# Interleaving the two halves of a split-precision weight block on the matrix engine

## The reference

```
for i in range(DEPTH):                      # 2 layers
    h = h + 0.5 * swiglu(rms_norm(h, norm_ff1[i]), gate, up, down)   # 1024 -> 2816 -> 1024
    hn = rms_norm(h, norm_mix[i])
    if i % 2 == 0:  # z, xbc, dt, gate, xb = split(hn @ hyb_w_in); SSD and RG-LRU; concat @ hyb_w_out
    ...
    else:           # q, k, v = split(hn @ dif_w_qkv); differential attention; @ dif_w_o
    ...
    h = h + 0.5 * swiglu(rms_norm(h, norm_ff2[i]), gate, up, down)
return rms_norm(h, final_norm)
```

## Time and profile before

| | |
|---|---|
| median of 3 runs | 1106.83 us (1105.61 to 1107.73) |
| the profiled execution: its time | 1106.83 us |
| the profiled execution: its span | 1105.0 us |
| granted clock of TensorE, mean | 0.988 |
| PE busy | 1067.4 us, 97% |
| PEld busy | 950.1 us, 86% |
| DVE busy | 824.6 us, 75% |
| ACT busy | 600.0 us, 54% |
| matmuls | 6671, each with a weight load |

### The profile page before, as it was taken

One profiled execution on the slowest core, in us unless ns is written; L12 is line 12 of the kernel. 1 busy time (PEld: TensorE's weight loads), 2 busy tenths in 40 slices (PEclk: granted clock), 3 DMA queues, 4 the chain that ended last, 5 costly groups with the idle time before them and its releaser, 6 DMA issues.

```text
span 1105.0 us, 18467 instructions
## 1 busy us (share of the span) xinstructions
PE 1067.4 (97%) x6671; PEld 950.1 (86%) x6671; DVE 824.6 (75%) x1157; ACT 600.0 (54%) x915; POOL 152.1 (14%) x149
## 2 busy tenths in 40 slices
PE   6999999998998999999999999999999889999996
PEld 4888888897887998888888888888988788888885
DVE  6888765699898768887666887766589677888753
ACT  5555553574877446555445555543536655555442
POOL 7000011102343330000021000012111050000011
PEclk9999999998999999999999999999999999999998
DMA  8666775454443656667655666675644336667661
GB/s 237 198 194 195 201 207 165 136 150 122 123 119 97 177 167 189 191 190 219 189 165 159 194 194 192 189 220 157 175 132 125 91 104 183 191 192 199 191 196 38
DMA packets 364308, 186.51 MB, mean 169 GB/s; under 512 B 5457, under 2 KB 363985, under 8 KB 364257
## 3 DMA queue, kind: packets, MB, share of 16 engines
q1 hardware_dynamic: 364000, 185.26, 59.0%
q0 software_dynamic: 256, 0.59, 0.2%
HBM read 184.78 MB, written 1.05 MB: 168 GB/s over the span
## 4 chain that ended last, share of the span: by engine, by line
PE 83%; DVE 11%; ACT 3%; issue 2%; DMA 0%; DVEq 0%; ACTq 0%; SPq 0%
PE psum L205 44%; PE psum L208 23%; PE psum L189 4%; PE psum L193 4%; PE psum L190 4%; DVE wlo L178 4%; DVE xn L278 1%; ACT arena L1378 1%; DVE arena L912 1%; PE psum L683 1%; DVE small L1483 1%; DVE arena L1462 0%; ACT xn L269 0%; DVE arena L1505 0%; DVE small L1500 0%
## 5 line engine op out<-in xcount | busy, mean ns | idle before, releaser
L178 DVE TENSOR_TENSOR wlo<-raw,whi 128x1024 fp32r<-128x1024 f32 (+1 forms) x324 | 427.5, 1339 | 62.6 <-ACT whi L173 61.7
L173 ACT ACTIVATE whi<-raw 128x1024 fp32r<-128x1024 f32 (+1 forms) x322 | 352.6, 1112 | 43.7 <-PE psum L193 41.9
L205 PE MATMUL psum<-xn,whi 128*128 128x512 f32 x1408 | 360.0, 396 | 11.5 <-ACT whi L173 7.9
L205 PEld LDWEIGHTS psum<-xn,whi 128*128 128x128 f32 x1408 | 255.4, 190 | 61.9 <-DVE xn L278 8.6
L208 PEld LDWEIGHTS psum<-xn,wlo 128*128 128x128 f32 x1408 | 192.9, 191 | 13.7
L208 PE MATMUL psum<-xn,wlo 128*128 128x256 f32 x1408 | 197.1, 283 | 0.0
L205 PE MATMUL psum<-hid,whi 128*128 128x512 f32 x704 | 172.1, 392 | 0.0
L205 PEld LDWEIGHTS psum<-hid,whi 128*128 128x128 f32 x704 | 128.1, 189 | 24.4 <-DVE hid L462 0.4
L189 PE MATMUL psum<-xn,whi 128*128 128x256 f32 x480 | 125.0, 297 | 0.9 <-DVE xn L278 0.9
L190 PE MATMUL psum<-xn,whi 128*128 128x256 f32 x480 | 120.3, 287 | 0.0
L189 PEld LDWEIGHTS psum<-xn,whi 128*128 128x128 f32 x480 | 93.9, 196 | 5.4 <-issue 3.4
(11 more groups left out here) (195 smaller groups left out, 1048.8 us busy)
## 6 DMA issues: line engine op xcount, KB each, us to landing
raw<-in_ffn_gate SPq DMA_DIRECT2D x88, 512.0 KB, 3.8
raw<-in_ffn_up SPq DMA_DIRECT2D x88, 512.0 KB, 4.0
raw<-in_ffn_down SPq DMA_DIRECT2D x64, 704.0 KB, 4.7
raw<-in_hyb_w_in SPq DMA_DIRECT2D x36, 512.0 KB, 4.2
raw<-in_dif_w_qkv SPq DMA_DIRECT2D x24, 512.0 KB, 4.5
raw<-in_hyb_w_out SPq DMA_DIRECT2D x16, 512.0 KB, 4.8
raw<-in_dif_w_o SPq DMA_DIRECT2D x8, 512.0 KB, 4.3
h<-in_xT SPq DMA_DIRECT2D x2, 512.0 KB, 5.2
```

The costliest lines, as they stand in the source:

```text
L173: act.activation(whi[:, s, 0:k * P], raw[:, s, 0:k * P], ACT.Copy).then_inc(s_whi, 1)
L178: dve.tensor_tensor(wlo[:, s, 0:k * P], raw[:, s, 0:k * P], whi[:, s, 0:k * P].bitcast(F32), ALU.subtract).then_inc(s_wlo, 1)
L205: pe.matmul(acc, hi[:, j, :], x[:, t, :, :], start=start and j == 0, stop=False)
```

## The change

In both functions the two loops over the k tiles become one. Tile by tile, the lo matmul now follows the hi matmul (in `multiply`, the two hi matmuls) of the same tile. One wait stands at the start of the block, for `s_wlo`; the wait for `s_whi` is gone, since the lo half of a block is made from its hi half. The number of matmuls, of weight loads and of their columns is unchanged, and nothing changes on the other engines. The order in which the products are added changes.

```diff
         def multiply(pe, b, s, k, x, k0, acc, start=True, stop=True, need=None, part=None):
-            hi, lo = tile_of(whi, s, k), tile_of(wlo, s, k)
-            pe.wait_ge(s_whi, b + 1)
+            pe.wait_ge(s_wlo, b + 1)
             for j in part or range(k):
                 t = k0 + j
                 if need:
                     need(t)
-                pe.matmul(acc, hi[:, j, :], x[:, t, 0, :], start=start and j == 0, stop=False)
-                pe.matmul(acc, hi[:, j, :], x[:, t, 1, :], start=False, stop=False)
-            pe.wait_ge(s_wlo, b + 1)
-            for j in part or range(k):
-                mm = pe.matmul(acc, lo[:, j, :], x[:, k0 + j, 0, :], start=False, stop=stop and j == k - 1)
+                w_hi, w_lo = tile_of(whi, s, k)[:, j, :], tile_of(wlo, s, k)[:, j, :]
+                pe.matmul(acc, w_hi, x[:, t, 0, :], start=start and j == 0, stop=False)
+                pe.matmul(acc, w_hi, x[:, t, 1, :], start=False, stop=False)
+                mm = pe.matmul(acc, w_lo, x[:, t, 0, :], start=False, stop=stop and j == k - 1)
             if j == k - 1:
                 mm.then_inc(s_blk, 1)

         def multiply_wide(pe, b, s, k, x, k0, acc, start=True, stop=True, need=None):
-            hi, lo = tile_of(whi, s, k), tile_of(wlo, s, k)
-            pe.wait_ge(s_whi, b + 1)
+            pe.wait_ge(s_wlo, b + 1)
             for j in range(k):
                 t = k0 + j
                 if need:
                     need(t)
-                pe.matmul(acc, hi[:, j, :], x[:, t, :, :], start=start and j == 0, stop=False)
-            pe.wait_ge(s_wlo, b + 1)
-            for j in range(k):
-                mm = pe.matmul(acc[:, T:2 * T], lo[:, j, :], x[:, k0 + j, 0, :], start=False,
-                               stop=stop and j == k - 1)
+                w_hi, w_lo = tile_of(whi, s, k)[:, j, :], tile_of(wlo, s, k)[:, j, :]
+                pe.matmul(acc, w_hi, x[:, t, :, :], start=start and j == 0, stop=False)
+                mm = pe.matmul(acc[:, T:2 * T], w_lo, x[:, t, 0, :], start=False, stop=stop and j == k - 1)
             mm.then_inc(s_blk, 1)
```

## The result

The changed kernel takes 1112.95 us (median of 8 executions, 1108.48 to 1117.98) against 1106.76 us before (1105.46 to 1107.75): a ratio of 1.0055 with a 95% interval of 1.0032 to 1.0079. It is slower by half a percent, where 1102.2 us and 0.4% faster was forecast, and 1112.95 lies above the range that was given. Its executions also differ much more among themselves: all 25 that were taken of it ran from 1107.1 to 1118.0. In the changed file, L206 and L207 are the wide hi and lo matmuls, L190 to L192 the narrow ones.

The account below looks back on a forecast made before the run. The prediction took PE's matmul stream, plus a few stalls at stage borders, to bound the kernel. Its terms, -4.9 + 5.1 - 3.3 - 1.0 - 0.5 = -4.6 us, gave 1102.2 us, 0.4% faster, with a range of 1088 to 1110.

Parts of the forecast that it names:

- The stream, wide blocks: Gate, up and down blocks of the ffn phases: a pair costs 0.3466 us when interleaved, 4.9 us less in all.
- settled and settled: Wide pair priced from the hi and lo steps of settled runs: 0.227 + 0.120 = 0.347 us.
- first and first: Wide pair priced from the first step of a hi run and of a lo run: 0.233 + 0.113 = 0.346 us.
- the prediction's own bounds: Wide pair between 0.340 us (14 us less than forecast) and 0.353 us (13.5 us more).
- the rival of the long steps: Every pair of the ffn phases pays hi 0.233 and lo 0.120: 13.5 us more, 1115.7 us; chance 0.20.
- The other two rivals: Wide stream: no change-over cost won back, pair 0.349, 1107.1 us, chance 0.13; short steps, pair 0.340, 1088 us, chance 0.17.
- The stream, narrow blocks: In hyb and att all three matmuls of a tile step by 0.120 in either order: costed at nothing.
- The wait at the start of a block: PE waits for the lo half at the first down blocks of each ffn phase: 5.1 us more, nothing elsewhere.
- Tile waits filled by lo matmuls: Lo matmuls fill activation waits: 3.3 us less at starts of phases, 1.0 us less at the mixers' output blocks.
- The start: First block's lo matmuls go into its activation waits and the second block starts earlier: 0.5 us less.
- The sum: Whole kernel: -4.9 + 5.1 - 3.3 - 1.0 - 0.5 = -4.6 us, 1102.2 us, 0.4% faster.

Follow-up runs that it names:

- profile after: Profiled execution of the changed kernel, to hold against the kernel before: 1112.92 us with a span of 1111.1, 6.1 more than before.
- serp: Against the kernel before, every second block in the loops of the down stages takes all lo, then all hi matmuls: 1105.94 us.
- narrow_only: Against the kernel before, only the narrow function (hyb and att) interleaved, with its wait for the lo half ahead: 1105.12 us, ratio 0.9972.
- wait_only: Matmul order of the kernel before, but each block in both functions waits for its lo half at its start: 1113.99 us, ratio 1.0064.
- borders: Against the kernel before, interleaved only in blocks that wait tile by tile for their activation, first down blocks excepted: 1102.1 us, ratio 0.995.

## Why the prediction was wrong

**The stream, wide blocks: the step that failed.** "Two combinations lie between and agree: settled and settled, 0.227 + 0.120 = 0.347, and first and first, 0.233 + 0.113 = 0.346. I take 0.3466." The step that failed is the choice of one price inside the bounds. The number is exact for one of two paces: 0.3466, gate blocks 2.773, down blocks 3.813, all as forecast. That is in part luck, since the steps of that pattern (233, 117, 231, 112 ns) are those of neither combination; only their sum is. The other pace, 0.3533, is the upper end of the prediction's own bounds, and two stages in three ran at it (22 of the 32 interleaved from their first block on). It holds a step that the settled stream of before doesn't have, a hi step of 241 ns. The reading of that stream was too simple as well: its hi steps are 233, 236, 228, 233 and 231 ns before they settle at 227, so 0.233 was neither the only long step nor the longest. For the profile after, the term is 2 x 44 x (-0.020) + 2 x 44 x 0.033 + 4 x 16 x 0.054 = +4.6 us, where -4.9 stood. These 9.5 us are most of the 10.7 between the forecast's difference and the profiled one; the rest is in the mixers, where hyb came out 3.3 us above its forecast and att 2.0 below, with their stretches at half clock in other places than before. With all eight stages at the fast pace the profiled execution would have taken some 1103.4 us (an estimate, 1112.92 - 9.5), near the forecast of 1102.2. The mean pair of that execution is 0.3511, beyond the 0.3488 that the rival of the long steps named as its point of decision. That rival had the price nearly right (0.353) and its place only in part: every pair of a slow stage, not of the whole kernel. The argument that two combinations agree was no evidence: both were sums of steps from a stream with long runs. The other two rivals fell: `serp` shows that the 0.020 us belong to the change-over and not to the border of blocks, and no stage ran below 0.3466 a pair.

**The stream, narrow blocks:** right. All three matmuls step by 0.120 in either order, and the narrow function alone makes the kernel faster (`narrow_only`).

**The wait at the start of a block:** right in place and in size: from start to start 5.2 us in after and 5.3 in `wait_only`, for 5.1. PE starts 0.10 us after the lo half is ready, where 0.05 was put in for the signal. That the second pair of down blocks needs no wait of its own held. That nothing else is paid held in the steady blocks of the profiles. `wait_only` is 7.1 us slower by its ratio, where the waits less the 0.8 of the start are 4.5; the second profile of it shows time at half clock in the mixers as what differs between executions, and leaves open why it costs more than in before.

**Tile waits filled by lo matmuls:** right. The first gate blocks went from 3.09, 3.57 and 4.83 us to 2.83, 2.83 and 4.00, 1.8 us less for 1.9 forecast. In the mixers `narrow_only` gives some 3 us for 2.4, with an interval of 1.8 to 4.3.

**The start:** 0.8 us less for 0.5: the fourth block starts at 23.77 instead of 24.63, and 0.06 of that is the pace. The clock rose earlier, the second block ran at full clock, and PE then waited 0.7 us for the squares of POOL ahead of the sums over tokens:

```profile
16.65 0.50 PE L206 MATMUL psum<-xn,whi 128*128 128x512 f32 x1 [0.93 <-DVE wlo L178]
...
20.45 0.70 PE L306 MATMUL psum<-sumsq,con 128*128 128x256 f32 x2 [0.72 <-POOL sumsq L292]
```

**The sum.** The terms of the forecast as measured give, with the stream first, +4.6 + 5.2 - 1.8 - 0.8 - 1.0 (both mixers together) = +6.2 for the 6.1 measured. `borders` keeps the three gains, leaves the stream and the waits, and lands at 1102.1 where 1102.0 to 1102.8 was expected.

**What stays open.** What in the engine makes two patterns, and what chooses between them. Shown is that a stage keeps its pace once the entry and, in a gate stage, the sums are behind it; that the first and third gate stage and the second down stage changed sides between two executions of the same program; and that it was the slow pace in 32 of 32 entries from the running stream of the old order. That the place in the pattern at which the stream is cut decides is a reading of 13 stages, not an experiment.

## What to carry to other kernels

Where an engine is the bound, filling its waits by reordering is worth doing exactly at the blocks that wait; the same reordering in the steady stream is a bet on the pace of a stream that no trace has shown yet. A price for such a stream made of steps of another stream should carry both ends as real cases, and one profile is not enough to see it: a spread between executions that is wider than before is itself a finding, once it is compared at equal granted clock. A stage-by-stage count of matmuls in equal windows shows such a thing at once.

## What the runs showed of the hardware

A stream in which matmuls of 512 and 256 columns alternate, each with its own weights, runs at full clock at 0.3466 or at 0.3533 us a pair, in fixed patterns of two or three pairs that last for more than 100 us (after, first and second gate stage). Long runs step by 0.227 and 0.120, and a change from a run of 256 columns to one of 512 costs 0.020 once (`serp`). The Trainium skill, "TensorE: Matmul & The Clock Gate", section "Back-to-back issue gap", gives for the gap of isolated matmuls the columns over 2.4 GHz plus 2.5 ns, which as an estimate would be 0.216 and 0.109, one value for each size. No run here has isolated ones; the steps in the streams of this case are longer in both orders, and for the same size they differ by the order around them (0.230 to 0.241 for 512 columns when interleaved).
